# Neighbourhood attention on one core: the first scores of each group moved ahead of a product with the values

## The reference

```
s_loc = jnp.einsum('bhrjqd,bhrjkd->bhrjqk', qb, kg).astype(jnp.float32) + bias[None]
s_loc = jnp.where(valid, s_loc, -jnp.inf)
s_ctx = jnp.einsum('bhrjqd,bhkd->bhrjqk', qb, k_ctx).astype(jnp.float32)
p = jax.nn.softmax(jnp.concatenate([s_loc, s_ctx], axis=-1), axis=-1).astype(v.dtype)
o = (jnp.einsum('bhrjqk,bhrjkd->bhrjqd', p[..., :nk], vg)
     + jnp.einsum('bhrjqk,bhkd->bhrjqd', p[..., nk:], v_ctx))
```

## Time and profile before

| | us |
|---|---|
| median of 3 runs | 3584.63 (3583.44 to 3585.93) |
| the profiled execution | 3581.11 |
| its span | 3579.3 |
| attention stage, first scores to the end | 2134.8 to about 2509 |
| one pair of heads in it | 45.10 |

### The profile page before, as it was taken

How to read it: one execution, slowest core, us unless ns; L and a number is a source line. 1 busy time by engine, 2 the same in 40 slices (tenths; PEclk the granted TensorE clock), 3 DMA queues, 4 the chain that set the end, 5 groups by cost and what they waited for, 6 DMA issues and landing times. The chain is left out here.

```text
span 3579.3 us, 47143 instructions
## 1 busy us (share of the span) xinstructions
PE 3467.5 (97%) x19104; PEld 3016.0 (84%) x19104; DVE 1514.4 (42%) x2557; ACT 1037.8 (29%) x1558; POOL 1243.0 (35%) x819
## 2 busy tenths in 40 slices
PE   8999999989999999999999998999999999999997
PEld 8988888778888888888888778888878888888886
DVE  6865535756244444434521116777151111111116
ACT  5521211335311111111442326777252111111113
POOL 6411117435322222222541315666252222222223
PEclk9999999999999999999999999999999999999998
DMA  4533328541222222222163457775211111111111
GB/s 178 186 121 121 115 83 277 182 176 63 67 71 71 65 66 72 75 77 70 64 217 149 164 158 178 176 175 124 100 36 36 42 36 40 37 36 42 37 41 65
DMA packets 173814, 365.92 MB, mean 102 GB/s; under 512 B 16967, under 2 KB 98439, under 8 KB 171944
## 3 DMA queue, kind: packets, MB, share of 16 engines
q1 hardware_dynamic: 168168, 352.55, 31.0%
q10 hardware_dynamic: 5440, 10.49, 0.9%
HBM read 285.38 MB, written 77.59 MB: 101 GB/s over the span
## 5 line engine op out<-in xcount | busy, mean ns | idle before, releaser
L148 POOL TENSOR_TENSOR w_lo<-w_raw,w_hi 128x1024 fp32r<-128x1024 f32 x207 | 504.2, 2436 | 1418.0 <-ACT w_hi L142 1417.8
L156 PE MATMUL ps_r<-a_hi,w_hi 128*128 128x512 f32 (+1 forms) x2496 | 887.8, 356 | 2.5 <-POOL a_lo L2006 1.8
L156 PE MATMUL ps_r<-a_lo,w_hi 128*128 128x512 f32 (+1 forms) x2496 | 885.2, 355 | 0.0
L156 PE MATMUL ps_r<-a_hi,w_lo 128*128 128x512 f32 (+1 forms) x2496 | 884.1, 354 | 0.0
L156 PEld LDWEIGHTS ps_r<-a_hi,w_hi 128*128 128x128 f32 x2496 | 472.5, 189 | 73.1 <-POOL a_lo L2006 6.1
L156 PEld LDWEIGHTS ps_r<-a_lo,w_hi 128*128 128x128 f32 x2496 | 472.5, 189 | 65.5 <-issue 1.0
L156 PEld LDWEIGHTS ps_r<-a_hi,w_lo 128*128 128x128 f32 x2496 | 472.2, 189 | 65.4
L142 ACT ACTIVATE w_hi<-w_raw 128x1024 fp32r<-128x1024 f32 x207 | 217.3, 1050 | 737.6 <-PE ps_r L156 541.0
L2215 DVE TENSOR_TENSOR hid_l<-hid_l,ps_r 128x1280 f32<-128x1280 f32 x44 | 65.4, 1487 | 824.7 <-PE ps_r L156 824.7
L2235 DVE SCALAR_TENSOR_TENSOR x_t_l<-ps_r,mod,x_t_l 128x1024 f32<-128x1024 f32 (+1 forms) x288 | 241.3, 879 | 260.3 <-PE ps_r L156 260.3
L156 PE MATMUL ps_front<-x_split_f,w_hi 128*128 128x512 f32 (+1 forms) x1152 | 307.8, 356 | 0.0
(11 more groups left out here) (257 smaller groups left out, 6061.9 us busy)
## 6 DMA issues: line engine op xcount, KB each, us to landing
w_raw<-in_w_all SPq DMA_DIRECT2D x205, 512.0 KB, 3.6
ada_w_l<-in_ada_t SPq DMA_DIRECT2D x59, 512.0 KB, 3.5
v_hl<-v_d SPq DMA_DIRECT2D x128, 128.0 KB, 2.9
t_tail_f<-in_ada_t SPq DMA_DIRECT2D x24, 512.0 KB, 4.1
spec<-gout_f SPq DMA_DIRECT2D x80, 128.0 KB, 2.1
g_spec_c<-spec ACTq DMA_DIRECT2D x20, 512.0 KB, 4.9
v_d<-z_v_l SPq DMA_DIRECT2D x10, 1024.0 KB, 4.5
q_hl_l<-q_d SPq DMA_DIRECT2D x32, 320.0 KB, 7.4
```

The lines of the kernel that those rows point to most:

```text
L148: pool.tensor_tensor(wl[:, s, 0:width], raw[:, s, 0:width], wh[:, s, 0:width].bitcast(F32), ALU.subtract).then_inc(w_split, 1)
L156: last = pe.matmul(out[:, c0:c1], w[:, c % 2, blk * 128:blk * 128 + 128], x[:, c0:c1], start=start and b == 0 and term == 0, stop=stop and ...
```

## The change

TensorE gets the scores of three units in the prologue, not two. In step g it transposes the first unit, issues the scores of unit 2g+3, transposes the second unit and the context part, issues the scores of unit 2g+4 (the first of the group after next) and then the product of group g-1. The other engines follow.

```
 # TensorE
-                    for half in range(2):
-                        if scored(g, last):
-                            scores(i, 2 * g + 2 + half)
-                        if local(2 * g) and not (last and g == G):
-                            turn_local(i, 2 * g + half)
-                    if not (last and g == G):
+                    turned = not (last and g == G)
+                    if turned and local(2 * g):
+                        turn_local(i, 2 * g)
+                    if scored(g, last):
+                        scores(i, 2 * g + 3)
+                    if turned and local(2 * g):
+                        turn_local(i, 2 * g + 1)
+                    if turned:
                         turn_ctx(i, g)
+                    if scored(g + 1, last):
+                        scores(i, 2 * g + 4)
                     if g:
                         mix(i, g - 1)
 # ScalarE
                     if turned and local(2 * g):
                         high_local(i, 2 * g)
+                        high_local(i, 2 * g + 1)
                     if scored(g, last):
-                        exps(i, 2 * g + 2)
-                    if turned and local(2 * g):
-                        high_local(i, 2 * g + 1)
+                        exps(i, 2 * g + 3)
                     if turned:
                         high_ctx(i, g)
-                    if scored(g, last):
-                        exps(i, 2 * g + 3)
+                    if scored(g + 1, last):
+                        exps(i, 2 * g + 4)
 # GpSimd
-                    for half in range(2):
-                        if not (last and g >= G - 2):
-                            bias_mask(i, 2 * g + 4 + half)
-                        if scored(g, last):
-                            norm(i, 2 * g + 2 + half)
+                    if scored(g, last):
+                        norm(i, 2 * g + 2)
+                    if scored(g + 1, last):
+                        bias_mask(i, 2 * g + 5)
+                    if scored(g, last):
+                        norm(i, 2 * g + 3)
+                    if scored(g + 2, last):
+                        bias_mask(i, 2 * g + 6)
 # VectorE
                     if scored(g, last):
-                        minima(i, 2 * g + 2)
+                        recip(i, 2 * g + 2)
                     if g >= 2:
                         out_low(i, g - 2)
+                    if scored(g, last):
+                        minima(i, 2 * g + 3)
                     if turned and local(2 * g):
                         low_local(i, 2 * g)
+                    if scored(g + 1, last):
+                        minima(i, 2 * g + 4)
                     if scored(g, last):
-                        minima(i, 2 * g + 3)
-                        recip(i, 2 * g + 2)
+                        recip(i, 2 * g + 3)
                     if turned and local(2 * g):
                         low_local(i, 2 * g + 1)
                     if turned:
                         low_ctx(i, g)
-                    if scored(g, last):
-                        recip(i, 2 * g + 3)
```

More of the change, by code:

```diff
@@ L2485, in prologue @@
                     pe.sem_inc(pv_mm, PV0)
-                    scores(0, 0)
-                    scores(0, 1)
+                    for u in range(3):
+                        scores(0, u)
                 def step(i, g, last):
-                    for half in range(2):
-                        if scored(g, last):
-                            scores(i, 2 * g + 2 + half)
-                        if local(2 * g) and not (last and g == G):
-                            turn_local(i, 2 * g + half)
-                    if not (last and g == G):
+                    turned = not (last and g == G)
[6 more added lines that the diff above has]
+                    if turned:
                         turn_ctx(i, g)
+                    if scored(g + 1, last):
+                        scores(i, 2 * g + 4)
                     if g:
@@ L2528, in prologue @@
                     act.activation(stat[:, 0, 3:4], eps[:, :], ACT.Exp)
-                    exps(0, 0)
-                    exps(0, 1)
+                    for u in range(3):
+                        exps(0, u)
                 def step(i, g, last):
@@ L2577, in prologue @@
                     norm(0, 1)
+                    bias_mask(0, 4)
                 def step(i, g, last):
-                    for half in range(2):
-                        if not (last and g >= G - 2):
-                            bias_mask(i, 2 * g + 4 + half)
-                        if scored(g, last):
-                            norm(i, 2 * g + 2 + half)
+                    if scored(g, last):
[6 more added lines that the diff above has]
+                        bias_mask(i, 2 * g + 6)
                 run(pool, prologue, step)
@@ L2629, in prologue @@
                     recip(0, 0)
+                    minima(0, 2)
                     recip(0, 1)
```

## The result

The changed kernel takes 3566.07 us (median of 5 runs, 3562.28 to 3571.56), the kernel before beside it 3585.62 us (5 runs, 3583.44 to 3587.49): a ratio of 0.9948, 95% interval 0.9935 to 0.9960. That is 19.5 us less, where 25 were forecast. The profiled execution has a span of 3564.3 us against 3579.3.

What follows compares the result with a forecast made beforehand. TensorE bounds kernel and stage, losing 5.5 us a pair to waits. Seven pairs 22.5, last pair's rest 1.5, first pair 1.0: 25 us, profiled 3581.1 to 3556, as median 3560 (chance 0.50); own range 3555 to 3565, whole range 3547 to 3572.

Steps and rivals of the forecast that it cites:

- clean head: One head of layer 1's attention stage without the late bias: 19.80 + 0.54 = 20.34 us forecast, a pair 40.68.
- TensorE's work, 19.80 a head in steps of 3.16, 4.55, 4.13, 4.04, 3.87: TensorE's time without waits in steps 0 to 4 of a head, claimed still 19.80 us in the new order.
- The first unit's wait and the low output's go: TensorE's waits for each group's first-unit probabilities (0.72 by starts in one case) and low outputs (0.9 a pair) vanish.
- The second unit's chain: From one step's second transposes to the next's, 3.69 us against TensorE's 3.15: a 0.54 wait per head, in step 1.
- The bias late by 1.2 a pair: Second head's bias load lands 1.6 us late, delaying step 4's context transposes: 1.2 us a pair, bounds 0 and 7.0.
- the first rival: Second head's bias is not late in the attention stage: gain 33 us, 3551 us; chance 0.22.
- VectorE's queue costs more: Bias sum ahead of GpSimd's normalisation: chain 4.57, step 1 wait 1.4; gain 12 to 18, about 3570 us; chance 0.17.
- nothing changes: In the attention stage, TensorE's waits are replaced by as many for VectorE's chains: 3585 us; chance 0.06.
- Slower: Second head's bias takes 12.9 us to land, 5.9 later: 41 us lost against the 25, 3601 us; chance 0.05.
- The first pair, 1.0: First pair's second head still waits for its first bias load; TensorE has 1.0 us more done there.
- The half clock of the first pair: TensorE at half clock (0.50) during the first pair's bias wait, from 2163 to 2167; the same counted for after.
- seven pairs: First pair's second head to the same place in the last: 3.22 us saved a pair, 22.5 in all.

## Why the prediction was right, and where its sizes were off

It was right in the mechanism and in the places of the waits: 3560 forecast, 3566 measured, inside the range and 1 us above the forecast's own range. What was off is a size, TensorE's time for a clean head.

- **TensorE's work, 19.80 a head in steps of 3.16, 4.55, 4.13, 4.04, 3.87.** From the starts between 2273.61 and 2294.16 the steps are 3.92 (step 4), 3.19, 5.20 less the wait of 0.60 = 4.60, 4.11 and 4.13: 19.95. (My five steps add to 19.75, not to 19.80; I had kept the total of the old order.) The new neighbours, for which I had no row and allowed 0.05 a step, thus cost 0.15 a head over the sum and 0.20 over the steps, most of it in step 3 (0.09).
- **The first unit's wait and the low output's go.** Both did: steady steps show neither; two waits for a low output are left in the last pair.
- **The second unit's chain, 3.69 against 3.15, a wait of 0.54 in step 1 alone.** It is 0.60. From the starts the chain is 2282.30 - 2278.50 = 3.80, against 3.20 of TensorE's own. The second chain over VectorE, through ps_l, I had not counted; it ends 0.45 earlier, so it cost nothing here, but it stood in the way of the swapped reciprocal.
- **A clean head, 20.34.** It is 20.58 from mark to mark: 0.15 from neighbours, 0.06 from the chain, the other 0.03 not traced. This is the term that was mis-sized: 0.24 a head, 0.48 a pair.
- **The bias late by 1.2 a pair.** 1.20 by the kernel with the early load, between 0.75 and 1.98 in single pairs. In the pair shown the bias sum began 0.9 later than I put the landing, and the head lost 1.79. The mean came out right, but that it did so to 0.1 is luck: I had taken it from one pair, and single pairs differ by 1.2. With this the first rival (bias on time, 33 us) is excluded for the change. The kernel with the early load is what it describes, and gains 29; most of what it lacks of 33 is the clean head again.
- **VectorE's queue costs more.** Excluded: one wait a head, 0.60 and not 1.4; GpSimd is through with the bias sum and stands 0.73 before that normalisation (2281.44); and the new orders of the engines other than TensorE are worth 0.56 a head. The rival *nothing changes* falls with it; what it described came about only where ScalarE was left behind. *Slower* needed a landing 3.6 over the 7.0 of the sum; in the pair shown the sum of the bias began 0.9 over it.
- **The first pair, 1.0.** By the cuts of the sum (the product that ends step 4 of a pair's first head) it is 0.7; the rows stand below. I named the bias load as the only fixed point. TensorE waits for the second head's keys too, and in the new order the first scores that need them stand ahead of the product of group 2, which was done before that wait in the old order (its last row is at 2157.62, the keys' scores at 2160.08). After, the product has to be done behind it, at half clock. What this costs is not shown: two more executions with the same loads and order up to there reach the same cut 34.0 and 36.7 us after the stage's start (the bias issued 2 us earlier, and the early bias), against 33.9 in the change. The spread is larger than the term.
- **The half clock of the first pair.** The earlier trace rows doesn't stand in GpSimd's wait for the bias, as I wrote, but behind it: the wait lasted from 2154.8 to 2162.1, and the granted clock, read in windows of 1 us, was 1.00 up to 2161 and 0.50 from about 2161.5 to 2168.3. Counting the same for after was right: 6.8 us at 0.50 in both.

The rows of TensorE that follow the product in the first and in the last pair, before and then after, with the two that follow the wait for keys in between:

```profile
2168.78 0.81 PE L2434 MATMUL ps_s<-k_hl,q_hl 128*128 128x256 f32 x6
...
2484.50 0.82 PE L2434 MATMUL ps_s<-k_hl,q_hl 128*128 128x256 f32 x6
```
```profile
2163.61 1.54 PE L2434 MATMUL ps_s<-k_hl,q_hl 128*128 128x256 f32 x6 [3.38 <-DMA k_hl<-k_d]
2164.95 0.52 PE L2479 MATMUL ps_o<-pt_hi,v_hl 128*128 128x256 f32 x1
...
2172.93 0.49 PE L2438 MATMUL ps_l<-ident,probs 128*128 128x128 f32 x3
...
2469.92 0.49 PE L2438 MATMUL ps_l<-ident,probs 128*128 128x128 f32 x3
```

In the new order the scores of the next unit (0.65) stand ahead of that product, so at the same cut the kernel after has them done. The shortfall of the stage, 25 - 20.8 = 4.2, is by these cuts:

| | before | after | gain | forecast |
|---|---|---|---|---|
| stage's start to the first cut | 33.96 | 33.88 | 0.08, and 0.65 of scores done ahead: 0.7 | 1.0 |
| seven pairs | 315.7 | 297.0 | 18.7 | 22.5 |
| last cut to the stage's end | 25.2 | 23.2 | 2.0, less those 0.65: 1.4 | 1.5 |

So 3.8 of the 4.2 lie in the seven pairs, 42.42 each instead of 41.88: 0.48 of the 0.54 are the two clean heads, the rest the late bias (1.26 as the mean of these seven). The remaining 1.3 between 20.8 and the 19.5 of the medians is within the spread of the rest of the program.

## What to carry to other kernels

When work on the bounding engine is moved, list every transfer with a fixed time that lies ahead of it, and compare each landing with the new, earlier need: the late bias took back 1.2 us a pair here, and moving the issues of bias and of the first pair's keys gave some 15 us where the change had given 19.5. Price each new pair of neighbours on the bounding engine too: 0.15 us a head was more than half of what the forecast of a clean head missed. An order written out for several in-order engines is one thing: leave one engine in the old order and the engine that waits for it holds back what stands behind, which cost the entire gain. Where a wait is small, look for the second chain, here 0.45 us behind in 3.8, before shortening the first.

## What the runs showed of the hardware

- The landing of the stage's first transfers varies between executions. With that part of the queue the same, the second head's keys let TensorE go on between 24.4 and 26.7 us after the stage's start in nine executions. TensorE arrives there after 23.1 in the two kernels with its old order, after 20.7 to 21.9 in six with the new one, and after 19.5 in the seventh (TensorE's order alone, the one execution whose stage began with 3.4 us at half clock, where the ten others have 10.2). So the waits are 1.4 and 2.2 us, and 3.4, 3.6, 3.8, 4.2, 4.6, 5.4 and 7.0. That is as much as the rest of an experiment is worth, so I read orders from the steady pairs.
- In all nine a stretch at half clock begins in that wait or up to 2.3 us behind it. Windows of 4 us in the first pair, of after, of the kernel with only the bias early, and of that with TensorE's order alone:

```profile
2163.00:2167.00 4.00, 3.39 (x16) 3.39 (x17) 0.00 (x0) 0.00 (x0) 1.03 (x2) 0.50 1.05 252
2167.00:2171.00 4.00, 4.00 (x28) 4.00 (x28) 3.28 (x9) 1.39 (x4) 3.31 (x6) 0.73 1.05 244
```
```profile
2163.00:2167.00 4.00, 1.55 (x7) 1.55 (x8) 0.00 (x0) 0.00 (x0) 0.00 (x0) 0.50 1.06 220
2167.00:2171.00 4.00, 4.00 (x20) 4.00 (x21) 2.03 (x6) 0.94 (x3) 3.35 (x5) 0.50 1.04 217
```
```profile
2163.00:2167.00 4.00, 2.87 (x14) 2.87 (x14) 0.00 (x0) 0.00 (x0) 0.79 (x1) 0.50 1.04 234
2167.00:2171.00 4.00, 4.00 (x29) 4.00 (x29) 2.14 (x6) 1.72 (x5) 2.74 (x5) 0.79 1.04 234
```

Its length doesn't follow the wait's. Added up from windows of 1 us, it is 6.8 us behind waits of 1.4, 2.2, 3.4, 3.6, 4.6 and 7.0, 3.4 us behind those of 3.8 and 4.2, and 10.2 behind that of 5.4.

In the first of these the scores behind the wait are drawn at 1.54 us (the row of 2163.61 above), where full clock shows 0.82 for the same six matmuls. The kernel with both loads moved, whose waits there are 1.6 and 1.2, is granted 1.00 from 2155 to 2175. A wait for a transfer can thus have a second price behind it, of 3.4 to 10.2 us at half clock in nine executions and of none in this one; what decides between them these runs don't show.
